# The second feed-forward block of an encoder layer: its first two weight units opened together

## What is computed

```python
x = x + 0.5 * swiglu(rmsnorm(x, ffn1_norm), ffn1_w_gu, ffn1_w_down)
x = x + token_mixing(rmsnorm(x, mix_norm), ...)
x = x + cross_attention(rmsnorm(x, xa_norm), rmsnorm(mem, mem_norm), wq, wkv, wo)
x = x + 0.5 * swiglu(rmsnorm(x, ffn2_norm), ffn2_w_gu, ffn2_w_down)
return rmsnorm(x, final_norm)

def rmsnorm(x, g):  return x * rsqrt(mean(x * x, -1) + EPS) * g
def swiglu(h, w_gu, w_down):
    gate, up = split(h @ w_gu, 2)          # 1024 -> 2 x 2816
    return (silu(gate) * up) @ w_down      # 2816 -> 1024
```

## Time and profile before

| what | value |
|---|---|
| time, median of 3 runs | 1185.71 us (1184.31 to 1186.06) |
| span of the profiled execution, first to last instruction | 1183.3 us |
| median of the runs less that span | 2.4 us |
| PE busy | 1144.0 us, 97% of the span |
| DVE, ACT, POOL busy | 45%, 36%, 42% |
| mean granted TensorE clock | 0.991 |
| HBM traffic | 95 GB/s over the span |

### The profile page before, as it was taken

How to read it: one execution, slowest core, us unless ns; L and a number is a source line. 1 busy time by engine, 2 the same in 40 slices (tenths; PEclk the granted TensorE clock), 3 DMA queues, 4 the chain that set the end, 5 groups by cost and what they waited for, 6 DMA issues and landing times.

```text
span 1183.3 us, 14737 instructions
## 1 busy us (share of the span) xinstructions
PE 1144.0 (97%) x5366; PEld 950.1 (80%) x5366; DVE 534.2 (45%) x660; ACT 428.6 (36%) x576; POOL 494.9 (42%) x208
## 2 busy tenths in 40 slices
PE   6999999999999999999998999998999999999997
PEld 4888888888887888787877888786888888888886
DVE  7433343442222567888478224456344334332222
ACT  6322332232222645554246543335232223222221
POOL 4444444444444333232325773134444444444440
PEclk9999999999999999999999999998999999999999
DMA  6323223223333222121222542122322322233312
GB/s 225 107 89 106 89 92 103 100 95 107 106 105 104 76 72 72 55 70 54 84 94 82 185 159 72 39 71 89 106 90 89 106 90 98 96 107 104 104 60 71
DMA packets 33317, 113.10 MB, mean 96 GB/s; under 512 B 3712, under 2 KB 5888, under 8 KB 33152
## 3 DMA queue, kind: packets, MB, share of 16 engines
q1 hardware_dynamic: 33136, 111.53, 27.9%
q10 hardware_dynamic: 144, 1.05, 0.3%
HBM read 110.47 MB, written 2.10 MB: 95 GB/s over the span
## 4 chain that ended last, share of the span: by engine, by line
PE 42%; issue 38%; POOL 16%; DVE 2%; ACT 1%; POOLq 0%; DVEq 0%; ACTq 0%
POOL wl L340 16%; PE bank L964 13%; PE bank L966 13%; PE bank L965 13%; DVE acc L642 1%; ACT xh L384 0%; DVE x L662 0%; PE score L964 0%; DVE x L956 0%; PE score L966 0%; PE score L965 0%; PE n_bank L1007 0%; POOLq L339 0%; PE o_bank L964 0%; ACT wh L352 0%
## 5 line engine op out<-in xcount | busy, mean ns | idle before, releaser
L340 POOL TENSOR_TENSOR wl<-raw,wh 128x1024 fp32r<-128x1024 f32 x204 | 494.7, 2427 | 662.0 <-ACT wh L352 349.2
L964 PE MATMUL bank<-xh,wh 128*128 128x512 f32 x952 | 378.0, 397 | 4.6 <-DVE xl L634 4.6
L966 PE MATMUL bank<-xh,wl 128*128 128x512 f32 x952 | 372.4, 391 | 0.0
L965 PE MATMUL bank<-xl,wh 128*128 128x512 f32 x952 | 372.4, 391 | 0.0
L365 ACT ACTIVATE wh<-raw 128x1024 fp32r<-128x1024 f32 x104 | 110.4, 1062 | 396.1 <-DVE ubuf L678 219.4
L964 PEld LDWEIGHTS bank<-xh,wh 128*128 128x128 f32 x952 | 179.9, 189 | 44.9 <-DVE xl L634 5.9
L965 PEld LDWEIGHTS bank<-xl,wh 128*128 128x128 f32 x952 | 180.0, 189 | 38.8 <-issue 2.0
L966 PEld LDWEIGHTS bank<-xh,wl 128*128 128x128 f32 x952 | 179.8, 189 | 38.0
L352 ACT ACTIVATE wh<-raw 128x1024 fp32r<-128x1024 f32 x99 | 104.3, 1053 | 140.0 <-PE bank L966 139.0
L964 PE MATMUL bank<-hid_h,wh 128*128 128x512 f32 (+1 forms) x374 | 141.0, 377 | 0.0
L966 PE MATMUL bank<-hid_h,wl 128*128 128x512 f32 (+1 forms) x374 | 140.8, 377 | 0.0
(11 more groups left out here) (209 smaller groups left out, 1081.7 us busy)
## 6 DMA issues: line engine op xcount, KB each, us to landing
raw<-w_all SPq DMA_DIRECT2D x204, 512.0 KB, 3.3
x<-x_t SPq DMA_DIRECT2D x8, 256.0 KB, 5.7
out_t<-x SPq DMA_DIRECT2D x8, 256.0 KB, 2.3
memf<-mem_t ACTq DMA_DIRECT2D x1, 1024.0 KB, 4.9
gbuf<-masks_d SPq DMA_DIRECT2D x1, 256.0 KB, 8.4
ident<-ident_d SPq DMA_DIRECT2D x1, 64.0 KB, 8.1
par<-params SPq DMA_DIRECT2D x1, 36.5 KB, 3.1
```

Source lines behind the costliest of these rows:

```text
L340: nc.gpsimd.tensor_tensor(wl[:, c, :], raw[:, c, :], wh[:, c, :].bitcast(f32), SUB)\
L964: nc.tensor.matmul(out_, a[0], b_[0], start=first, stop=False)
L965: nc.tensor.matmul(out_, a[0], b_[1], start=False, stop=False)
L966: return nc.tensor.matmul(out_, a[1], b_[0], start=False, stop=last)
```

## The change

In the second block's opening, units 0 and 1 are worked on together, in two banks: k-tiles 0 to 6 of unit 0, k-tiles 0 to 6 of unit 1, then k-tile 7 of unit 0, k-tile 7 of unit 1, and then the sum of squares. Every matmul of before is there, with the same operands and into the same bank; each bank's k-tiles keep their order. The waits of `group` are repeated at each part: `lo_ready` and `group_read` of the unit, and `x_lo` at every k-tile, now for unit 1 as well. `unit_used` is still incremented at the end of each unit, unit 0 first. No other engine's program is changed.

```diff
                 else:
-                    group(u0, g0, x_phase=ph)
+                    for ks in (range(KC - 1), range(KC - 1, KC)):
+                        for c in range(2):
+                            pe.wait_ge(lo_ready, u0 + c + 1)
+                            pe.wait_ge(group_read, g0 + c + 1)
+                            for k in ks:
+                                pe.wait_ge(x_lo, KC * ph + k + 1)
+                                last = product(bank[(g0 + c) % 4][:, :], wpair((u0 + c) % SLOTS, 128 * k, 128 * k + 128),
+                                               (xh[:, k, :], xl[:, k, :]), k == 0, k == KC - 1)
+                            if k == KC - 1:
+                                last.then_inc(unit_used, 1)
                     sum_squares(norm, qn + KC)
-                    group(u0 + 1, g0 + 1)
                 for c in range(2, 4):
                     group(u0 + c, g0 + c)
```

## The result

| | before | changed |
|---|---|---|
| median | 1185.87 us (1184.31 to 1186.06, 4 runs) | 1178.11 us (1177.57 to 1178.55, 4 runs) |
| span of the profiled execution | 1183.3 us | 1176.3 us |
| mean granted clock of it | 0.991 | 0.993 |

The ratio is 0.9934, 95% interval 0.9916 to 0.9951: faster by 7.8 us, which the interval makes 5.8 to 10.0. The forecast was 1179.0, in a range of 1177.3 to 1181.6. (The before column has one run more than the table ahead of the prediction, whose median of 1185.71 the forecast starts from.)

A forecast was written before the change was run, and what follows sets the result against it. PE, busy 97% of the span, bounds the kernel, losing time at the seam. 4.12 us of pause and 2.59 of clock make 6.71, so 1185.71 - 6.7 = 1179.0 us, range 1177.3 to 1181.6.

The forecast's parts named there:

- The pause and its filling: PE ahead of unit 0's k-tile 7: 21 matmuls of unit 1 fill the 4.12 us pause, leaving no idle time.
- The sum of squares: PE behind unit 1: takes 0.86 us at full clock instead of 1.70, its last square ready 1.45 us ahead.
- The start of unit 2: PE after the sum of squares: unit 2 starts at 817.53 in place of 824.24, 6.71 us earlier.
- The clock's term: Half-speed stretch behind the pause, 814.67 to 824.24: filling the idle time keeps the clock up and saves 2.59 us.
- The rival of a smaller term: Behind the seam's pause: the clock costs only 1.25 us in the common execution, time 1180.3 us; chance 0.12.
- counts of 6, 11 or 14: Slow matmuls after a rest, differing between runs, cited from the Trainium skill; clock's term then 1.2 to 2.8 us.
- The norm's slack: Unit 0's bank, read by 821.51, is first wanted by unit 4 at 828.40: 6.9 us to spare.
- The weights of units 4 and 5: POOL's `wl` pieces come before their uses at 828.40 and 833.84, slack 8.5 and 5.7 us: no wait.
- The pause doesn't reappear at unit 4: Answers the rival that the pause only moves to unit 4 and nothing is gained, 1185.7 us; chance 0.03.
- the release of unit 0 didn't move: Answers the rival that unit 0's release, now behind 21 matmuls, delays the norm, time over 1188; chance 0.04.
- The clock doesn't fall: Answers the rival that the clock falls at the seam all the same, gain 4.1, time 1181.6 us; chance 0.05.
- The last addition: Rival on DVE: k-tile 7 or its square late; last addition, if stretched, 0.71 us late, time 1179.7; chance 0.05.

The follow-up runs named there:

- e2: Kernel before in its order, with 18 matmuls into a bank nobody reads put ahead of unit 0's k-tile 7: 1183.36 us, ratio 0.9985.
- e3: Changed kernel with the second block's sum of squares behind unit 2 in place of unit 1: 1179.40 us, ratio 0.9945.
- e4: Changed kernel with the second block's sum of squares behind unit 3 in place of unit 1: 1182.29 us, ratio 0.998.
- e8: Changed kernel run once more, unchanged: 1178.94 us, ratio 0.9952.
- e7: Kernel before run once more, unchanged, with another execution profiled: 1185.86 us (11 runs) and 1185.72 us (17 runs).
- e1: Changed kernel with only k-tiles 0 to 2 of unit 1 in the pause, 3 to 7 after unit 0's k-tile 7: 1181.93 us, ratio 0.9967.
- e5: Kernel before, with VectorE adding the square of tile m behind xl of tile m + 1, PE's order untouched: 1179.16 us, ratio 0.9946.

## Why the prediction was right

- **The pause and its filling.** `xl[7]` was to be there 0.64 us before PE. In the changed trace it is ready at 814.26 and PE comes at 814.99: 0.73. 21 matmuls were put at 4.76 us; they take 4.80 (810.19 to 814.99).
- **The sum of squares** at full clock: 0.86 us forecast, 0.87 measured. Its operand was there long before, at 814.86.
- **The start of unit 2.** Forecast 817.53. Measured 816.35 + 0.87 = 817.22, in an execution whose seam lies 0.35 us earlier (`xl[7]` at 813.51 against 813.86): 817.57 on the old scale.
- **The clock's term** of 2.59 us: no slow stretch is left. e2 measures the term alone at 2.1 us by the medians (0.6 to 3.1) and at 2.4 and 2.2 by the timelines of the two profiled executions of the kernel before. The rival of a smaller term, 1.25 us, lies within the medians' interval but fits neither of these executions. The 11 slow matmuls that the prediction counts in the window are 10; the eleventh, at 819.89, is the first at full pace. Its counts of 6, 11 or 14 are for the start of a kernel and not for a pause within one; behind this pause the two executions show 10 and 9.
- **The norm's slack**, 6.9 us: the bank of unit 0 is read by 821.04 and unit 4 starts near 828.1 (817.22 + 10.88), 7.1 us. e3 and e4 bracket it.
- **The weights of units 4 and 5**: POOL's rows end at 819.47 and, for two pieces together, at 827.94; the uses are near 828.1 and 833.5. The first of the two pieces, unit 5's, is out by about 825.3, an estimate (half of the row). No wait.
- **The rivals.** The pause doesn't reappear at unit 4, and the release of unit 0 didn't move: ACT starts on it at 815.93, 0.48 us earlier than before, 0.35 of which is the earlier seam. The clock doesn't fall. The last addition takes 0.68 us, unstretched.
- **What came beside it.** The two profiled spans differ by 7.0 us, 0.35 of it ahead of the seam, which leaves 6.65 for the seam against 6.71 forecast. The first medians differ by 7.8, those of e8 by 6.8. The excess of the first is not explained by the seam; clock falls in other stages differ between executions by as much (e7 and e1: 1.7 us for one such stretch). So the forecast of 1179.0 came within 0.9 us of the median and within 0.1 of e8's, and the sum itself is tested by the 6.65 us of the timelines.

## What to carry to other kernels

Read an in-order engine's pause together with the pace of what follows it: here 4.1 us of waiting cost another 2.2 to 2.6 us through the half speed behind it, and even useless matmuls in the gap won that second part. To fill such a gap, look for work whose operands are all there and whose results nobody awaits, and work out how long what it is put ahead of can wait (e3, e4). And look at who is late: the same pause went away by putting one engine's less urgent operation behind its urgent one, without touching the engine that waited.

## What the runs showed of the hardware

- A pause of 2.01 us left the clock at 1.00 (e1), one of 2.82 us too (the window behind e4's pause, below), while 2.71 us in the mixing stage were followed by a slow stretch, in all twelve traces of this case (pauses of 2.70 to 2.72 us), and 3.95 us by one of 5.2 us. Near 404 us the wait ahead was 1.34 us in e1 and in the kernel before alike, and the clock fell in e1 alone. The length of the pause alone doesn't decide.

```profile
831.00:836.00 5.00, 5.00 (x22) 4.15 (x23) 4.12 (x4) 3.02 (x4) 3.37 (x2) 1.00 0.00 0
```

- A VectorE operation with two operands in SBUF and a POOL piece exclude each other, as the rows read; no run here moved POOL's pieces to test it. The addition that starts at 809.62 inside POOL's piece of 809.49 to 811.91 ends at 812.47, 0.56 us behind the piece, and takes 2.85 us where 0.69 is usual; in e5 the addition at 797.57, which starts ahead of the piece of 797.75, keeps 0.68 and the piece takes 2.77, and line 662 at 798.17, one of whose operands is a bank, keeps 0.68 inside the piece. `xl` is stretched in the same way (1.72 us at 807.98 before, beside 0.75 at 813.86). The Trainium skill (SBUF — State Buffer, "Who interferes with whom") states the exclusion as a lock, held for a whole instruction by whichever of the two starts first; the trace agrees. The prediction had the long addition as a given; that its place in the order decides about 0.9 us for each tile, and with it the whole pause, it had not seen.
